# Stick-breaking attention on one core: values of two pairs projected together, masks by a resetting running sum, one function table, out-projection begun beside the last pair

## The reference, cut to what matters

```python
q, k, v = [split_heads(t, N_HEADS) for t in jnp.split(x @ w_in, 3, axis=-1)]
qb, kb, vb = blocks(q * ATTN_SCALE), blocks(k), blocks(v)      # ATTN_SCALE = 1/8
strict = a[None, :] < a[:, None]
suffix = (a[:, None] >= a[None, :]).astype(jnp.float32)
z = jnp.clip(jnp.einsum('bhnqd,bhnkd->bhnqk', qb, kb), -SB_CLIP, SB_CLIP)
sp = jnp.where(strict, jnp.log1p(jnp.exp(z)), 0.0)
r_in = jnp.einsum('bhnqj,js->bhnqs', sp, suffix)
att = jnp.where(strict, jnp.exp(z - r_in), 0.0)
acc_d = jnp.einsum('bhnqs,bhnsd->bhnqd', att, vb)
...
zz = jnp.clip(jnp.einsum('bhqd,bhkd->bhqk', qblk, kblk), -SB_CLIP, SB_CLIP)
rr = jnp.einsum('bhqj,js->bhqs', jnp.log1p(jnp.exp(zz)), suffix)
pv = jnp.einsum('bhqs,bhsd->bhqd', jnp.exp(zz - rr), vblk)
acc = acc + jnp.exp(-r_sum)[..., None] * pv
...
return merge_heads(o.astype(x.dtype)) @ w_out
```

## Time and profile before

| | us |
|---|---|
| median of 3 runs | 2251.47 |
| lowest, highest | 2247.94, 2253.26 |
| the profiled execution | 2251.17 |
| its span in the trace | 2249.5 |

### The profile page before, as it was taken

How to read it: one execution, slowest core, us unless ns; L and a number is a source line. 1 busy time by engine, 2 the same in 40 slices (tenths; PEclk the granted TensorE clock), 3 DMA queues, 4 the chain that set the end, 5 groups by cost and what they waited for, 6 DMA issues and landing times.

```text
span 2249.5 us, 34445 instructions
## 1 busy us (share of the span) xinstructions
PE 2083.7 (93%) x14390; PEld 1755.2 (78%) x14390; DVE 1393.1 (62%) x1824; ACT 1061.6 (47%) x1156; POOL 21.6 (1%) x36
## 2 busy tenths in 40 slices
PE   6999988998997899889999888999999998888998
PEld 6999976777896688668879757688788887575886
DVE  3554545776786577676664575766666645756665
ACT  3444444565565466545553242555555443415553
POOL 1000000000000000000000000000000000000000
PEclk9999999999998999999999999999999999899999
DMA  6444422787221278725554220355455543112552
GB/s 233 143 161 159 172 82 113 287 315 286 85 95 64 113 298 317 272 84 196 180 211 144 100 84 4 137 177 188 168 189 179 192 169 131 39 49 87 179 191 103
DMA packets 41613, 358.63 MB, mean 159 GB/s; under 512 B 4767, under 2 KB 4911, under 8 KB 7328
## 3 DMA queue, kind: packets, MB, share of 16 engines
q1 hardware_dynamic: 38272, 341.86, 41.3%
q0 software_dynamic: 3232, 15.20, 2.2%
HBM read 355.92 MB, written 1.12 MB: 159 GB/s over the span
## 4 chain that ended last, share of the span: by engine, by line
PE 78%; DVE 11%; ACT 5%; DMA 3%; DVEq 2%; issue 1%; SPq 0%; ACTq 0%
PE psum L466 14%; PE psum L735 14%; PE psum L467 14%; PE psum L468 14%; PE psum L737 7%; PE psum L2226 2%; DMA ring<-moe_w 2%; PE psum L682 2%; PE psum L1333 1%; DVE ring_lo L480 1%; PE psum L1310 1%; PE psum L1319 1%; ACT ring_hi L474 1%; PE psum L2042 1%; DVE ring_lo L906 1%
## 5 line engine op out<-in xcount | busy, mean ns | idle before, releaser
L480 DVE TENSOR_TENSOR ring_lo<-ring,ring_hi 128x3072 fp32r<-128x3072 f32 (+1 forms) x124 | 407.6, 3287 | 169.0 <-ACT ring_hi L474 169.0
L735 PE MATMUL psum<-xT_both,ring_hi 128*128 128x512 f32 x1408 | 501.9, 399 | 2.0 <-DVE xT_both L564 1.7
L737 PE MATMUL psum<-xT_both,ring_lo 128*128 128x256 f32 x1408 | 395.2, 281 | 0.0
L474 ACT CAST ring_hi<-ring 128x3072 fp32r<-128x3072 f32 (+1 forms) x124 | 334.6, 2700 | 14.5 <-DVE oT L2542 13.8
L735 PEld LDWEIGHTS psum<-xT_both,ring_hi 128*128 128x128 f32 x1408 | 264.5, 188 | 70.9 <-issue 3.5
L737 PEld LDWEIGHTS psum<-xT_both,ring_lo 128*128 128x128 f32 x1408 | 265.9, 189 | 3.0
L468 PE MATMUL psum<-xT_both,ring_lo 128*128 128x256 f32 x896 | 253.8, 283 | 0.0
L906 DVE TENSOR_TENSOR ring_lo<-ring,ring_hi 128x2048 fp32r<-128x2048 f32 x96 | 218.7, 2285 | 42.8 <-ACT ring_hi L901 42.5
L901 ACT CAST ring_hi<-ring 128x2048 fp32r<-128x2048 f32 x96 | 183.8, 1916 | 73.3 <-DMA ring<-moe_w 73.3
L777 ACT COPY scratch<-psum 128x512 f32<-128x512 f32 x88 | 51.7, 588 | 312.9 <-PE psum L737 312.9
L468 PEld LDWEIGHTS psum<-xT_both,ring_lo 128*128 128x128 f32 x896 | 172.2, 192 | 0.0
(11 more groups left out here) (422 smaller groups left out, 3846.3 us busy)
## 6 DMA issues: line engine op xcount, KB each, us to landing
ring<-ff_w SPq DMA_DIRECT2D x88, 1536.0 KB, 6.5
ring<-moe_w SPq DMA_DIRECT2D x96, 1024.0 KB, 7.0
ring<-mix_w SPq DMA_DIRECT2D x20, 1536.0 KB, 6.6
ring<-dil_qk SPq DMA_DIRECT2D x24, 1024.0 KB, 4.9
ring<-proj_w SPq DMA_DIRECT2D x16, 1024.0 KB, 4.9
ring<-dil_v SPq DMA_DIRECT2D x8, 1536.0 KB, 6.5
ring<-sb_w SPq DMA_DIRECT2D x8, 1536.0 KB, 7.1
scratch<-rel_dram POOLq DMA_DIRECT2D x16, 384.0 KB, 4.6
```

The costliest lines, as they stand in the source:

```text
L474: nc.scalar.copy(ring_hi[:, s, 0:floats], ring[:, s, 0:floats]).then_inc(high_ready, 1)
L480: nc.vector.tensor_tensor(ring_lo[:, s, 0:floats], ring[:, s, 0:floats], ring_hi[:, s, 0:floats].bitcast(F32), ALU.subtract).then_inc(low_ ...
L735: nc.tensor.matmul(psum[:, bank, :].rearrange("p (w n) -> p w n", w=2), ring_hi[:, s, cols], xT_both[:, :, k, :], start=(k == 0), stop=False)
L737: last = nc.tensor.matmul(psum[:, bank, 0:SEQ], ring_lo[:, s, cols], xT_hi[:, k, :], start=False, stop=(k == KC - 1))
```

## The change

1. **Units regrouped, V of two pairs together.** The weights of a couple of pairs (2j, 2j + 1) lie in two units: unit 2j holds q and k of pair 2j and q of pair 2j + 1, unit 2j + 1 holds k of pair 2j + 1 and v of both. `project_v(j, t)` makes V of both pairs for one token tile t, in 24 matmuls of 256 columns; the two halves stand behind `weigh` of two successive pairs. `sb_v` holds two couples. `ring_free` of an even unit is given in `weigh` of the odd pair.
2. **Masks by the running sum.** `sb_mask` and the instructions L1657 and L1667 are gone. The running sum starts from 1e30 and is multiplied by 0 at the first key that a query may see, so that masked places keep 1e30 and their exp is 0.
3. **Scale.** The factor 1/8 is applied where the norm's transposed rows are copied out of PSUM (ACT with a scale, DVE `scalar_tensor_tensor`), for the side that makes q. `clip` is two instructions instead of three.
4. **Tables.** `preload_act_table_set("natural_log_exp_and_others")` at the stage's begin.
5. **Moves between engines.** The copies of V (now one for a couple) and of the output go from DVE to ACT. `weigh` waits for both heads' copies once, and takes the heads in turn.
6. **Pair 0 and pair 7.** `scores(0)` comes ahead of V's projection. The out-projection is in `pe_sticks`: units 0 and 1 for token tile 0 run after `weigh(6)`, then turn 7, unit 2, weigh 7, then tile 1 of units 0 to 2, and last unit 3 for tile 0 and for tile 1. The halves `act_output` and `dve_output` of units 0 to 2 are written around pair 6 (ACT in the step of pair 5).

```diff
+    couple = np.stack([np.stack([q[:, 0], k[:, 0], q[:, 1]], 3), np.stack([k[:, 1], v[:, 0], v[:, 1]], 3)], 1)
...
+                for k in range(KC):
+                    tok, cols = slice(t * P, (t + 1) * P), slice(k * 384 + P, k * 384 + 3 * P)
+                    last = products(psum[:, 1, t * SEQ:(t + 1) * SEQ], xTr_hi[:, k, tok], xTr_lo[:, k, tok],
+                                    ring_hi[:, s, cols], ring_lo[:, s, cols],
+                                    start=(k == 0), stop=(k == KC - 1))
...
             project_qk(0)
-            project_v(0)
             scores(0, 0); scores(0, 1)
             project_qk(1)
-            project_v(1)
-            for p in range(PAIRS):
-                if p + 1 < PAIRS:
-                    scores(p + 1, 0); scores(p + 1, 1)
-                turn_att(p, 0); turn_att(p, 1)
+            project_v(0, 0)
+            project_v(0, 1)
+            for p in range(PAIRS - 1):
+                scores(p + 1, 0); scores(p + 1, 1)
+                turn_att(p)
                 if p + 2 < PAIRS:
                     project_qk(p + 2)
-                weigh(p, 0); weigh(p, 1)
+                weigh(p)
                 if p + 2 < PAIRS:
-                    project_v(p + 2)
+                    project_v((p + 2) // 2, p % 2)
+            out_slots = pe_ring.take(4)
+            out_products(0, 0)
+            out_products(0, 1)
+            turn_att(PAIRS - 1)
+            out_products(0, 2)
+            weigh(PAIRS - 1)
+            for u in range(3):
+                out_products(1, u)
+            out_products(0, 3)
+            out_products(1, 3)
...
+            for p in range(1, PAIRS):
+                chain(p, p + 2)
+                if p == PAIRS - 2:
+                    dve_output(0)
+                    dve_output(1)
+            dve_output(2)
+            split(PAIRS + 2)
             split(PAIRS + 3)
+            dve_output(3)
...
-                if p + 1 == PAIRS:
-                    for u in range(3):
-                        act_output(u, o_copied, PAIRS + PAIRS - 1)
+                take_o(p)
+                if p + 2 == PAIRS - 1:
+                    act_output(0, o_copied, PAIRS + 2)
+                    act_output(1, o_copied, PAIRS + 4)
                 split(p + 4)
+                if p % 2 and p + 2 < PAIRS:
+                    take_v((p + 1) // 2)
+                if p + 2 == PAIRS - 1:
+                    act_output(2, o_copied, PAIRS + 6)
```

More of the change, by code:

```diff
@@ L345, in build_kernel @@
         sb_qk = carve(0, 2, 2 * SEQ)
-        sb_v = carve(1024, 2, SEQ)
+        sb_v = carve(20480, 2, 2, SEQ)
         sb_z = carve(1536, 2, 3 * P)
@@ L596, in act_norm @@
                     nc.scalar.wait_ge(turned, u.turned)
-                    if gain is None:
-                        last = nc.scalar.copy(x_hi[:, 2 * b:2 * b + 2, :].rearrange("p c n -> p (c n)"),
-                                              psum[:, 4 * side + b, :])
+                    flat = x_hi[:, 2 * b:2 * b + 2, :].rearrange("p c n -> p (c n)")
+                    if flip and side == 0:
+                        last = nc.scalar.activation(flat, psum[:, 4 * side + b, :], ACT.Copy, scale=SB_SCALE)
+                    elif gain is None:
+                        last = nc.scalar.copy(flat, psum[:, 4 * side + b, :])
                     else:
@@ L1611, in weigh @@
-                if a == 1:
-                    last.then_inc(o_ready, 1)
+                        for a in range(2):
+                            at = kt * P + a * HD
+                            last = pe.matmul(psum[a * HD:(a + 1) * HD, out_bank(p), t * P:(t + 1) * P],
+                                             sb_v[:, j % 2, side, at:at + HD], sb_aT[:, a, b * P:(b + 1) * P],
+                                             start=(n == 0), stop=(n == len(blocks) - 1))
+                            if side and t == 0 and a == 0 and p + 2 < PAIRS:
+                                last.then_inc(ring_free[slots[(p + 1) % SLOTS][0]], 1)
```

185 lines of the change are left out of this document (99 added, 86 removed).

## The result

| | before | changed |
|---|---|---|
| median, us | 2251.94 (4 runs) | 2229.1 (4 runs) |
| lowest, highest | 2247.94, 2253.26 | 2224.88, 2234.21 |
| the profiled execution | 2251.17 | 2234.21 |
| its span in the trace | 2249.5 | 2232.6 |

The ratio is 0.9894, with a 95% interval from 0.9869 to 0.992: 1.06% faster, and the interval leaves out 1. The forecast was 2224 with a range of 2217 to 2232. Both kernels were timed once more, the changed one in four runs and the kernel before in seven: 2226.16 against 2253.74, a ratio of 0.9878 (0.9862 to 0.9895).

What follows compares the result with a forecast made beforehand. The prediction took TensorE to bound the kernel, and circle B through VectorE the changed pair loop. Gains of 19.9 us up to pair 7's clip and 7.9 at the end, less 0.5, give 27.3: 2251.2 to 2224, range 2217 to 2232.

Steps and rivals of the forecast that it cites:

- Circle B: Pair loop: waits from scores through VectorE and ScalarE's copy of q and k; 13.84 us before, 12.0 after, the longest.
- TensorE keeps the pace: Rival, pair loop: ScalarE and VectorE 0.6 us quicker, six pairs at 11.34, total 2220; chance 0.13.
- Circle A: Pair loop: waits from scores through ScalarE's exp and ln and weigh; 14.53 us before, 9.78 after, 11.07 with table loads.
- TensorE's own work: Pair loop: weigh 1.09, V 2.92, scores and turn 1.50, q and k 5.83, together 11.34 us a pair.
- The start: Pairs 0 and 1: scores ahead of V and wider V bring clip of pair 1 5.1 us sooner.
- The steps of pairs 2 and 3: Clip to clip early in the loop: 12.4 us to pair 2, behind unit 3's split, then 12.0 to pair 3.
- ScalarE comes late: Rival, pair loop: ScalarE's split ends after VectorE wants it, 6 us more, 2230; chance 0.20 shared with the end rival.
- the end gives nothing: Rival, end: half clock lasts or tile 0's sum is late, 6 of 7.9 go, 2230; 0.20 shared with late ScalarE.
- The end: From clip of pair 7 to the normalised rows: 40.6 us against 48.5, so 7.9 gained.
- 2.9 given back: End: last tile's products end closer to the first's than VectorE's norm can follow, losing 2.9 us.
- +0.5: Behind the out-projection: fillers between the norm's transposes may run at half clock, 0.5 us added, ends -1.5 and +1.5.
- rival of 2283: Rival, pair loop: TensorE's clock falls to half from waits before the scores, loop grows by 59 us; chance 0.03.

Runs made afterwards that it cites:

- pair0_late: Changed kernel with V of the first couple projected ahead of pair 0's scores, as in the kernel before; 2230.55 us, one run.
- v_narrow: Changed kernel with V of a couple made in products of 128 columns, 96 instead of 48 of 256; 2240.38 us, one run.
- projection_last: Changed kernel with the whole out-projection behind turn and weigh of pair 7, as in the kernel before; 2226.26 us, one run.
- no_shared_table: Changed kernel without the preloaded common exp and ln table, so ScalarE loads two tables a pair; 2231.22 us, one run.
- tile0_sooner: Changed kernel with ScalarE's last out-projection split ahead of pair 7's copies and tile 0's unit 3 behind one tile 1 unit; 2228.93 us, ratio 0.9883.

## Why the prediction was right, and where it was not

**What bounds the pair.** Right. Circle B was put at 12.0 and the steps came at 11.92 to 11.97. The wait that the prediction asked for, 0.6 in front of the scores and ended by the copy of q and k, is there as 0.60. Taking that copy out of the circle freed all of it, so the rival "TensorE keeps the pace" falls: it came only with that edit. Putting VectorE's instructions back gave 13.84, which is the circle's sum. Circle A is a different matter. With the tables back the steps stayed at 11.96, as forecast, but the prediction's 11.07 for that case left out ScalarE's own list (the split and the copy of V stand ahead of exp): the margin was 0.17 in every second pair, not 0.9. There the forecast was right with less room than it thought.

**TensorE's own work** was put at 11.34 and measures 11.30; the nearness is luck, from errors against each other. Weigh was taken at its row of 1.09 and takes 0.80 with the heads in turn. V and the projection of q and k were taken 0.15 and 0.10 too short: the product behind a change of form has a pitch of about 0.2 instead of 0.12 (640.96 to 641.18; 646.19 to 646.39), and gaps of 0.09 stand in front of the scores and of weigh. None of it mattered, since TensorE wasn't the bound.

**The start.** Right to 0.04 and to 0.00: clips of pairs 0 and 1 at 23.24 and 35.80. The prediction has one figure of 5.1 for the order and for V; without the new order 2.3 of it go (pair0_late), without the wide V 4.9 (v_narrow), so neither part has a share that is its own.

**The steps of pairs 2 and 3** were put at 12.4 and 12.0 and came at 12.20 and 12.32, 0.1 more in the sum. The late split of unit 3 is there: VectorE's part starts at 611.61, when ScalarE's (608.80 + 2.77) ends, 0.22 later than its own clip would allow. The step after it has a cause that the prediction left out: TensorE waits for the copy of q and k 0.83 and 0.96 in those two pairs instead of 0.60, and in the second VectorE's running sum starts 0.43 late without a releaser in the trace. What that is stays open.

**ScalarE comes late** had 0.20 together with "the end gives nothing", for 6 more us, and did not come. Its margin held: from pair 4 on there is no wait of VectorE's split for ScalarE's in the steady part; ScalarE's part ends 0.29 before VectorE's starts (656.77 + 2.77 against 659.83). Where V's projection came first at pair 0 (pair0_late), a wait of 1.51 appeared once; so the mechanism was real and the margin small.

**The end.** 40.6 forecast, 40.65 measured, and the moments between within 0.3. What the prediction says is won, idle time around the last transposes and weigh and its half-clock part, is there: behind clip 7 TensorE was idle for 6.20 + 2.67 + 0.90 + 2.00 = 11.8 before and for 5.2 now. What it does not say is which edit takes it away, and a reader would think of the moved projection. By projection_last, that one gives 5.3 at TensorE's end and, less what VectorE's norm gives back, 2.6 at the end of the stretch. The other 5.3 of the 7.9 need no moved projection; 1.6 of them go with the tables in the changed kernel (no_shared_table; 0.4 in the kernel before), and the rest lies in the output halves made ahead, in the shorter weigh and in fewer products at half clock, which were not taken apart by runs. "2.9 given back" was right, and tile0_sooner got 3.2 of it.

**Half clock and filler.** Weigh 6 took 1.48 up to the next product instead of 2.00, and six products went at half clock, as forecast. The +0.5 that were added for the fillers between the norm's transposes did not show: they ran from 717.54 in 4.05 for 18, at full clock. The prediction's bound of -1.5 to +1.5 held it.

**One table.** Worth nothing in the loop up to pair 6 and 2.05 from there on; forecast 0 and 2. An exp, or ln, of the shared table takes 614 ns against 613, so the term for the function's duration is 0. The Trainium skill says the same in "ScalarE activation tables: per-element evaluation and per-set limits", section "What a function is on this engine"; the trace agrees.

**The clock.** The window over the loop of the changed kernel has 1.00, with waits of 0.60 to 0.96 in front of the scores of pairs 2 to 6:

```profile
606.00:681.00 75.00, 71.40 (x618) 65.97 (x617) 57.14 (x81) 47.46 (x73) 0.53 (x1) 1.00 0.35 127
```

So the rival of 2283 did not come. The Trainium skill, "TensorE: Matmul & The Clock Gate", section "A second HAM failure mode: psum-queue depth-cycling", tells of a bf16 kernel in which short idles between groups of matmuls made the clock swing; for idles of this size and distance the traces here don't show it.

**The total.** 27.3 were forecast: 27.8 in the stretch, less 0.5 for the transposes behind it. 27.8 came in the profiled stretch; the medians moved by 22.8 in the first set and 27.6 in the second, whose intervals overlap. The profiled execution's 10.2 above the forecast are the 10.9 outside the stretch, less the 0.5 that the forecast had put there. The prediction named this as a sign of a wrong sum (the stages behind take another time), and in that execution it came. For the median, 5.1 above it, the runs without a profile can't be placed like that. The prediction took 3.5 for that from three runs of before; the changed kernel's four runs lay 9.3 apart.

## What to carry to other kernels

Where two circles run beside each other with nearly the same length, work each out from the rows; a cut in one is worth only the distance to the next, and two cuts that are worth next to nothing alone (0.1 or less here, by the estimate above) can be worth 1.9 a pair together. Sum each engine's own list as well as the circles: the margin for the table loads was 0.17 and not 0.9. Then ask which copy closes the circle that is left, and whether the engine that makes it has it in the right place of its list: moving one line of ScalarE's order was worth 0.67 a pair. And when an end gains, put one part back before saying which part it was.

## What the runs showed of the hardware that was not expected

Twelve matmuls with 64 stationary columns each take 0.80 until the next product begins (647.03 to 647.83) when successive ones write the outputs of different heads, in different halves of the partitions, and 1.07 (647.70 to 648.77) with one head after the other, same shapes, same clock. That they overlap in the array is the likely reading; the runs show only the time. At half clock (0.50 in both windows) the row of twelve is 1.55 long with the heads in turn and was 2.00 before (686.88 and 705.57).

Between 128 and 256 columns the width of a product hardly counts: its pitch is 0.113 with 128 in v_narrow and 0.12 with 256.

The spread outside a stage that was changed (2072.9 to 2086.2 for the same work) is nearly half of what this change brings. Comparing the spans of the first two profiles puts the change at 17 us, comparing their stretches at 28.
